# An mLSTM and differential-attention step on one core: queries projected with stationary weights, the other four groups together, the sample rows' cell as a ninth tile

## The reference, cut to what matters

```python
p = rmsnorm(x, g) @ w_in                       # 1024 -> 5*1024 + 16
q, k, v, o, z, gi, gf = jnp.split(p, ...)      # 8 heads of 128 columns in each group
# per head and chunk, exact per token:
a   = jnp.exp(d - mj[..., None]) * jnp.einsum('bhjd,bhsd->bhjs', qc, kc)
num = w_inter[..., None] * jnp.einsum('bhvk,bhjk->bhjv', c, qc) + jnp.einsum('bhjs,bhsv->bhjv', a, vc)
h   = num / jnp.maximum(jnp.abs(den), jnp.exp(-mj))[..., None]
c_new = decay[..., None, None] * c + jnp.einsum('bhs,bhsv,bhsk->bhvk', wg, vc, kc)
hc = head_rmsnorm(jax.nn.sigmoid(o) * hc, hnorm)
y  = (hc * jax.nn.silu(z)) @ w_out             # x + y, c_new, n_new and m_new are outputs
```

## Time and profile before

| | us |
|---|---|
| median of 3 runs (1985.13 to 1988.81) | 1986.25 |
| the profiled execution, its own time | 1984.68 |
| its span | 1982.8 |
| TensorE busy in the span | 1762.5 (89%) |
| VectorE busy | 1082.4 (55%) |
| ScalarE busy | 821.3 (41%) |
| GpSimd busy | 350.4 (18%) |

### The profile page before, as it was taken

How to read it: one execution, slowest core, us unless ns; L and a number is a source line. 1 busy time by engine, 2 the same in 40 slices (tenths; PEclk the granted TensorE clock), 3 DMA queues, 4 the chain that set the end, 5 groups by cost and what they waited for, 6 DMA issues and landing times. The chain is left out here.

```text
span 1982.8 us, 33940 instructions
## 1 busy us (share of the span) xinstructions
PE 1762.5 (89%) x10531; PEld 1508.1 (76%) x10531; DVE 1082.4 (55%) x2801; ACT 821.3 (41%) x2040; POOL 350.4 (18%) x823
## 2 busy tenths in 40 slices
PE   4399999999999958699899999999999678888698
PEld 4399999999999946477887887887788566666486
DVE  4444534434435435534477676677666466666453
ACT  5233333333333312314355554555555356656322
POOL 1021212212212212101012222222212100101101
PEclk8699999999999966699899999999999798989799
DMA  4213032032131023414222112112101376776713
GB/s 125 67 33 69 2 66 44 23 68 36 32 68 15 1 63 92 147 50 137 60 58 64 41 53 63 45 49 61 37 26 32 115 252 224 269 252 239 249 68 110
DMA packets 160780, 173.83 MB, mean 88 GB/s; under 512 B 15178, under 2 KB 128682, under 8 KB 160674
## 3 DMA queue, kind: packets, MB, share of 16 engines
q1 hardware_dynamic: 156370, 168.30, 28.4%
q0 software_dynamic: 1184, 4.23, 0.8%
q10 hardware_dynamic: 3120, 0.01, 0.1%
HBM read 142.94 MB, written 29.56 MB: 87 GB/s over the span
## 5 line engine op out<-in xcount | busy, mean ns | idle before, releaser
L815 PE MATMUL PS<-WH,XH 128*128 128x384 f32 (+3 forms) x1152 | 369.3, 321 | 3.0 <-DVE WORK L737 3.0
L815 PE MATMUL PS<-WH,XL 128*128 128x384 f32 (+3 forms) x1152 | 356.7, 310 | 0.0
L815 PE MATMUL PS<-WL,XH 128*128 128x384 f32 (+3 forms) x1152 | 356.6, 310 | 0.0
L815 PEld LDWEIGHTS PS<-WH,XH 128*128 128x128 f32 (+1 forms) x1152 | 207.8, 180 | 7.9 <-DVE WORK L737 3.4
L815 PEld LDWEIGHTS PS<-WL,XH 128*128 128x128 f32 (+1 forms) x1152 | 208.2, 181 | 4.0
L815 PEld LDWEIGHTS PS<-WH,XL 128*128 128x128 f32 (+1 forms) x1152 | 207.4, 180 | 4.6
L2012 PE MATMUL PS<-W,XH 128*128 128x512 f32 x384 | 123.8, 403 | 0.0
L2438 PE MATMUL PS<-cst,RAW 128*128 128x128 f32 x512 | 86.5, 320 | 41.9 <-DVE XL L2345 36.5
L1766 ACT ACTIVATE WORK<-PD,WORK 128x896 f32<-128x896 f32 (+7 forms) x128 | 94.9, 742 | 62.5 <-DVE WORK L1933 57.5
L2438 PEld LDWEIGHTS PS<-cst,RAW 128*128 128x128 f32 x512 | 67.8, 163 | 59.7 <-DVE XL L2345 43.3
L2345 DVE TENSOR_TENSOR XL<-PS,XH 128x512 fp32r<-128x512 f32 x128 | 83.9, 684 | 38.3 <-ACT XH L2266 38.2
(11 more groups left out here) (381 smaller groups left out, 4278.9 us busy)
## 6 DMA issues: line engine op xcount, KB each, us to landing
RAW<-in_cache_k SPq DMA_DIRECT2D x64, 512.0 KB, 4.7
WORK<-in_cache_v SPq DMA_DIRECT2D x64, 512.0 KB, 4.4
RAW<-in_w_in_a SPq DMA_DIRECT2D x40, 512.0 KB, 6.3
out<-RAW SPq DMA_DIRECT2D x16, 512.0 KB, 3.2
RAW<-in_w_in_b SPq DMA_DIRECT2D x60, 128.0 KB, 2.4
RAW<-in_w_kv SPq DMA_DIRECT2D x56, 128.0 KB, 2.3
WORK<-in_x_prompt SPq DMA_DIRECT2D x8, 512.0 KB, 4.6
WORK<-d_G SPq DMA_DIRECT2D x8, 512.0 KB
```

Of the source, the lines that this page charges most:

```text
L815: last = nc.tensor.matmul(bank[0:rows, 0:n], x[:, k, tt], reg(w)[:, k, :], start=(i == 0), stop=(i == 3 * KT - 1))
```

## The change

It touches the gates stage, `mlstm_phase` and oa; the whole of `mlstm_sample_phase` goes.

- Queries are projected with the weights stationary: 128 columns of weights stay in the array and the activations of all 1056 rows stream in three chunks of 352 (`project_queries`, L999). The result is `QT`, queries already turned. So per head 3 x 24 matmuls of 352 columns.
- Keys, values, output gate and z are projected together: activations stationary, 24 matmuls of 512 columns per prompt tile (`project`, L1016). For the sample tile high and low activations stand side by side as 64 columns (`A_XS`), so 16 matmuls of 512 (L1020); ScalarE moves the low half's result to `TL` and VectorE adds the two.
- The sample rows' cell runs per head in the same loop, as tile 8. Its TensorE work stands between the halves of the next head's query chunks; after the last head it stands alone. The state is read into one buffer, updated in place and stored from it by SP.
- The wide weight cuts (8 of 512 columns, ScalarE L695 and VectorE L886) are made while the next head's queries are projected; the query weights (8 of 128 columns, L689 and L881) during the tiles.
- Finished rows are written in row order into `X1` (L876), so that `YT`, the per-tile transposes and `d_smA` go. oa now turns rows as ob does.
- Gates stage: one query load and four wide loads are issued where two loads were; the stage waits for them at its end.

Loads of a head's weights, and the loop over the heads (the body of head h also does the sample rows of head g = h - 1):

```diff
-        def load_qk_weights(sp, h, loaded):
-            for j in range(2):
-                sp.dma_start(qk_weights(RAW)[:, :, j * P:(j + 1) * P],
-                             w_in_a[0, :, bass.ds(j * D + h * P, P)].rearrange("(k p) c -> p k c", p=P)).then_inc(loaded, 16)
+        def load_q(sp, h, loaded):
+            sp.dma_start(wq(RAW), w_in_a[0, :, bass.ds(h * P, P)].rearrange("(k p) c -> p k c", p=P)).then_inc(loaded, 16)
+        def load_kvoz(sp, h, loaded):
+            for j in range(4):
+                sp.dma_start(wkvoz(RAW)[:, :, j * P:(j + 1) * P],
+                             w_in_a[0, :, bass.ds((j + 1) * D + h * P, P)].rearrange("(k p) c -> p k c", p=P)).then_inc(loaded, 16)
```

```diff
+            def heads(eng, body, links=None, per=0):
+                body(0, True, False)
+                with eng.Fori(1, H - 1) as h:
                     if links:
...
+                        links.enter(h - 1, per)
+                    body(h, False, False)
                 if links:
...
+                    links.leave(H - 2)
+                body(H - 1, False, False)
+                body(H, False, True)
```

ScalarE, the start of the body (what follows is the loop over the tiles), then VectorE at the same place:

```diff
+                    def body(h, first, last):
+                        g = h - 1
+                        if not first:
+                            inter(g, NT - 1)
+                            sigmoid(g, NT)
+                        if not last:
+                            for k in range(0, 3):
+                                cut(h, k)
+                        if not first:
+                            squares(g, NT - 1)
+                            tail(g)
+                            exponential(g, NT)
+                            keys_turned(g, NT)
+                            states(g, 0)
+                        if not last:
+                            queries(h, 0)
+                            for k in range(3, 6):
+                                cut(h, k)
+                        if not first:
+                            states(g, 1)
+                        if not last:
+                            queries(h, 1)
+                            for k in range(6, KT):
+                                cut(h, k)
+                            queries(h, 2)
+                        if not first:
+                            inter(g, NT)
+                            squares(g, NT)
+                        if last:
+                            return
```

```diff
+                    def body(h, first, last):
+                        g = h - 1
                         if not first:
...
+                            sample_rows(g)
+                            attend(g, NT - 1)
+                            carry(g, NT - 1)
+                            mask(g, NT)
+                            sample_weights(g)
+                            norm_column(g, 0)
+                            gate(g, NT - 1)
+                            output(g, NT - 2)
                         if not last:
...
+                            for k in range(0, 3):
+                                cut(h, k)
+                        if not first:
+                            ratio(g, NT - 1)
+                            gate(g, NT)
+                            attend(g, NT)
+                            sample_values(g, 0)
+                            output(g, NT - 1)
+                            dve.wait_ge(cev, h)
+                        if not last:
+                            v.memset(CA, 0.0).then_inc(ca, 1)
+                            for k in range(3, 6):
+                                cut(h, k)
+                        if not first:
+                            norm_column(g, 1)
+                        if not last:
+                            for k in range(6, KT):
+                                cut(h, k)
+                        if not first:
+                            ratio(g, NT)
+                            new_state(g, 0)
+                            sample_values(g, 1)
+                            new_state(g, 1)
+                            output(g, NT)
```

TensorE, the two projections and the body:

```diff
+                    def project_queries(h, c, ks):
...
+                        for k in ks:
+                            for i, (w, x) in enumerate(((WH, XH), (WL, XH), (WH, XL))):
+                                last = nc.tensor.matmul(PJ[c % 2][:, 0:CH], wq(w)[:, k, :], x[:, k, cc],
+                                                        start=(k == i == 0), stop=(k == KT - 1 and i == 2))
+                        if KT - 1 in ks:
...
+                    def project(h, t, ks):
...
+                                for i, (x, w) in enumerate(((XH, WH), (XH, WL), (XL, WH))):
+                                    last = nc.tensor.matmul(bank, x[:, k, tok(t, P)], wkvoz(w)[:, k, :],
+                                                            start=(k == i == 0), stop=(k == KT - 1 and i == 2))
+                            else:
+                                for w in (WH, WL):
+                                    last = nc.tensor.matmul(bank[0:2 * TS, :], XS[:, k, :], wkvoz(w)[:, k, :],
+                                                            start=(k == 0 and w is WH), stop=(k == KT - 1 and w is WL))
```

```diff
+                    def body(h, first, last):
+                        g = h - 1
+                        if not last:
+                            project_queries(h, 0, A)
                         if not first:
...
+                            within(g, NT - 1)
+                            tail(g)
+                            turn_keys(g, NT)
+                            turn_states(g, 0)
+                        if not last:
+                            project_queries(h, 0, B)
+                        if not first:
+                            scores(g, NT)
+                        if not last:
+                            project_queries(h, 1, A)
+                        if not first:
+                            past(g, 0)
+                            turn_states(g, 1)
+                        if not last:
+                            project_queries(h, 1, B)
+                        if not first:
+                            within(g, NT)
+                        if not last:
+                            project_queries(h, 2, A)
+                        if not first:
+                            past(g, 1)
+                        if not last:
+                            project_queries(h, 2, B)
+                        if not first:
+                            update(g, 0)
+                        if not last:
+                            project(h, 0, A)
+                        if not first:
+                            update(g, 1)
+                        if last:
+                            return
+                        project(h, 0, B)
+                        for t in range(1, NB):
+                            project(h, t, A)
+                            turn_keys(h, t - 1)
+                            if t >= 2:
+                                within(h, t - 2)
+                            project(h, t, B)
+                            scores(h, t - 1)
+                            carry(h, t - 1)
```

The first output stage turns its rows, and the sample stage is gone:

```diff
-                    if not first:
-                        turn_y(0)
-                        turn_y(1)
+                    turn_y(0)
+                    turn_y(1)
                     for i in range(2):
                         for t in range(NT):
                             project(i, t)
-                            if not first and i == 0 and t + 2 < NT:
+                            if i == 0 and t + 2 < NT:
                                 turn_y(t + 2)
-                            if not first and (i, t) == (0, 6):
...
         run(norm_phase)
         run(gates_phase)
         run(mlstm_phase)
-        run(mlstm_sample_phase)
         run(out_phase, "oa", w_out_a, True)
```

More of the change, by code:

```diff
@@ L558, in mlstm_phase @@
-            pj_free, tr_mm, tr_free = two("a_pjf"), two("a_tr"), two("a_trf")
-            dch, pch, ones_set = sem("a_dve"), sem("a_pool"), sem("a_ones")
-            B_S, B_IN, B_X, B_C = BK[4], BK[5], BK[6], BK[7]
-            def heads(eng, sweep1, sweep2, tail, links=None, per=0):
-                sweep1(0, None)
-                with eng.Fori(0, H - 1) as h:
+            U = take(2, P)
+            dn, rd, ssq, var, rs, rr2 = (take(2) for _ in range(6))
+            CA, CS = take(P + 2), take(P + 2)
@@ new lines, in update @@
+                    def update(h, half):
+                        pe.wait_ge(vw, 2 * h + half + 1)
+                        if half == 0:
+                            pe.wait_ge(cte, 2 * h + 2)
+                        else:
+                            pe.wait_ge(cn, 2 * h + 1)
+                        for j in range(4):
+                            x = nc.tensor.matmul(B_T[:, j * P:(j + 1) * P], VW[0:TS, j, :], keys(NT), start=True, stop=True)
+                        x.then_inc(upd, 1)
+                    A, B = range(0, KT // 2), range(KT // 2, KT)
@@ L1163, in out_phase @@
             XS = phase_tensor(f"{tag}_XS", [P, KT, 2 * TS], F32R)
```

(6 more changed lines are left out.)

927 lines of the change are left out of this document (400 added, 527 removed).

## The result

The changed kernel takes 1903.9 us (median of 4 runs, 1898.7 to 1907.2) against 1987.5 for the kernel before in the same runs: ratio 0.9576, 95% interval 0.955 to 0.9602. Forecast 1896, range 1866 to 1932. The profiled execution is the fastest of the four: 1898.74 us, span 1896.6.

A forecast was written before the change was run, and what follows sets the result against it. TensorE's stream sets the prompt's mLSTM stage; the sample stage behind it ran at clock 0.62. The profiled 1984.7 us, less 93.6 for the earlier first output-stage load, plus 5.1 for oa's turning, gave 1896.2, said as 1896; range 1866 to 1932.

The forecast's parts named there:

- three signs of being wrong: Tiles over 7 us apart; boundary under 18 or over 25 us; stretch behind the last head far from 27.
- Projections and tiles: Inside each head: eight prompt tiles of 6.67 us and the sample projection of 3.7, together 57.0 us.
- that rival: Prompt tiles: TensorE waits 0.5 us in each of 64, 32 us, giving 1928; chance 0.16.
- The boundary's work: Between heads, TensorE's own work: 11.4 us of query matmuls, 5.5 for 50 passes, 0.5 for seven breaks; 17.4 us.
- The first wait: Boundary between heads: TensorE waits 3.1 us at the sample tile's scores, ends 0 and 5.
- The second wait: Boundary between heads, last state update: TensorE has 2.8 us to lay over some 3.4, so it waits 0.6.
- the rival: Boundaries: the clock falls behind the wait, 12 to 25 us in seven boundaries, giving 1915; chance 0.20.
- row against the rival: Earlier trace: behind a gap of 3.48 us the clock stayed at 1.00; behind 2.88 it was 0.50.
- The ends: mLSTM stage: first matmul at 90.0, first head's queries done at 103.5, 27 us behind the last head.
- The formula beside the sum: Matmul issue gap: columns divided by 2.4 GHz plus 2.5 ns; saves 3.0 us a head instead of 3.9.
- The slower rival: Boundary at 1.2 GHz throughout: 17.4 us more in each of seven, 2018; decided from 12.6 us lost per boundary; chance 0.03.
- The other rival: Boundary between heads: ScalarE and VectorE keep up, no wait, 7 x 3.7 us less, 1870; chance 0.15.

The follow-up runs named there:

- the cell done apart: Changed kernel with the sample rows' cell done in one piece ahead of the next head's queries on TensorE, ScalarE and VectorE: 1973.2 us, ratio 0.9952.
- both early: Changed kernel with the ratio ahead of VectorE's three wide cuts and the exponential and turned keys ahead of ScalarE's squares: 1875.6 us, ratio 0.9459.
- The filled wait: Changed kernel with TensorE turning the identity 16 times while it would wait for the turned keys: 1886.1 us, ratio 0.9506.
- either link broken: Changed kernel with only the ratio ahead of VectorE's cuts, 1877.2 us, or only the exponential and turned keys ahead of ScalarE's squares, 1876.2 us.
- halves: Each 512 wide tile matmul split into two of 256: 1912.9 us on the changed kernel; 1882.3 with ratio and keys early, against 1875.6.
- ends: Norms turned behind the first twelve query matmuls, norms' store not waiting for states' store: 1902.1 us on the changed kernel, 1871.8 with ratio and keys early.

## Why the prediction was right, and where it was off

The cause was as forecast: the sample stage's 103 us and its stage change go into a stream that TensorE fills anyway, and with the cell done apart nearly all of the gain is gone. None of the three signs of being wrong came: tiles are 6.6 us apart, the boundary is 22.4 us on average, and behind the last head it takes 24.2. The sizes, by the prediction's own steps:

- **Projections and tiles.** 57.0 us a head forecast. With no wait and no clock loss a head is 75.50 us, of which the boundary is 19.1 (below), so 56.4. The tiles wait for nothing in the table of waits, so that rival is out.
- **The boundary's work.** 17.4 forecast, 19.1 measured: from the first query matmul to the first wide one, and the second state update, in the kernel with both early. A run of twelve query matmuls takes 2.08 us instead of 1.91, because behind a small step the first one is 0.24 to 0.27 us from the next, not 0.16, and the last is mostly 0.24 us from the small step behind it; six runs make 12.5 us. The 50 passes with their breaks take 6.6, not 6.0. This is the term that was most mis-sized, 12 us over seven boundaries.
- **The first wait.** 3.1 us, for the turned keys, behind the squares, behind the ratio, behind VectorE's cuts: measured 2.2 to 2.3, with each link shown by an experiment. The cuts took 0.64 and 0.69 us each (0.7 taken), and TensorE starts the scores 7.3 us behind the first query matmul instead of 8.1. The prediction counts 12 passes ahead of the scores where the order has 8; it reached them at 5.2 us all the same (5.0 forecast), since the runs of twelve took longer.
- **The second wait.** 0.6 us at the last state update: not there. L1100 has no bracket between heads.
- **The clock.** Taken as nothing in the forecast and as 12 to 25 us in the rival. In the profiled execution it is 7.8 us over six boundaries (474.6 us for six heads, against 453.0 without wait, less 13.8 of waits). The filled wait gives the same for the boundaries, 7.6 us. So the rival's mechanism was there too, beside the forecast and not in its place, and cheaper than its 12 us at the least: the median of 1903.9 lies between the forecast's 1896 and the rival's 1915. It fits that the median is 5 us above the profiled execution, whose mean clock was 0.941 against 0.935 to 0.938 in the other three. Whether these falls also make the runs spread isn't shown: the changed kernel's runs spread over 8.5 us, those of kernels with the wait gone over 2.0 to 6.8, and with the wait filled over 6.9. The prediction's row against the rival was weak: behind the gap of 3.48 us it looked at 0.8 us only. From 706.0 on the clock was 0.50, with TensorE nearly idle, and in the kernels here it fell up to 1.6 us behind the end of a wait. So that row doesn't show that the clock stayed. The Trainium skill (TensorE: Matmul & The Clock Gate, section HAM oscillation — how this bites in real kernels) puts the price of a fall at half of the time spent at the lower level. The rows come near it, a little below: 6.8 us low (401.4 to 408.3) cost 3.0, and 3.4 low behind 244.2 cost 1.5.
- **The ends.** First query matmul at 88.7 (90.0 forecast), first wide one at 102.9 (103.5), from the last tile to oa's first load 24.2 us (27).
- **The formula beside the sum.** The prediction says that its rows lie 4 to 16 ns a matmul above the formula of the Trainium skill that it cites. Worked out again from the earlier trace rows it is 10 to 16: 10 at 256 and 352 columns, 12.5 at 384, 16 at 512. The sum goes by the rows, so nothing hangs on it.
- **Sum, of the profiled execution.** The start is 0.6 us early, eight heads of tiles 4.8 less, seven boundaries 9.1 more (22.4 instead of 21.1: work 1.7 more, clock 1.1 more, the first wait 0.9 less, the second 0.6 less), the end 2.8 less: oa's first load at 735.1 for 734.2. oa's turning costs 4.2 us (56.9 less 52.7) for 5.1; another 2.3 us came in later stages, which the change doesn't touch. In the kernels here the stretch behind that load took 1159 to 1165 us with the same instructions, so 2.3 is within its noise. The median lies 5 us above this sum.

The nearness to 1896 is in part luck: a boundary too cheap by 1.3 us against tiles and an end too dear. The slower rival needed 12.6 us lost per boundary. The cell done apart loses 13.5 against no wait and 11 against the forecast's head, and it lands at 0.9952, so that point was well placed; what keeps the changed kernel away from it is the order.

The other rival, no wait at the boundary at 1870, is what the engines could have given: with either link broken the kernel takes 1876. It failed here only by the order on two engines that were busy less than half of the time.

## What to carry to other kernels

Where a short chain passes from engine to engine beside a full TensorE, look at what stands in each queue ahead of the link, not at how busy the engine is: three cuts and a squaring, which the scores don't need, cost some 23 us, and either of two moves of a line or two gave it back. Price a wait of TensorE by its length and by the clock behind it; here the second was 1.5 to 3.0 us wherever the clock fell, at waits from 1.67 us on, about half of the waits' own price over the changed kernel's boundaries, and nothing at 1.0. And measure small edits on a base in which the clock is steady: on the changed kernel the split's price couldn't be told from the clock's; with both moves in, its 6 us stood out. The edits at the ends stayed unclear on both.

## What the runs showed of the hardware

- The clock fell behind waits of 1.67 us in a stream that was busy before and after, in five of five boundaries, and behind 1.73 to 2.34 us in 16 of 21 (changed, halves, ends). Behind 1.5 us and less it held in every profiled boundary of the kernels with the cell interleaved. The fall came between 0.8 us before and 1.6 us behind the end of the wait, so a short window behind a gap can miss it, as the one of 0.8 us behind the 3.48 us gap does.
- Useless transposes of the identity in the gap kept it at 1.00 in all seven boundaries: 7.6 us gained there, and some more behind the last head, by work that computes nothing.
- Weight loads of 0.188 us hid behind matmuls of 256 columns that are 0.118 us apart; two such cost 6 ns more than one of 512.
